# Differential attention on one core: five units in flight instead of two, with zero-padded 128-row queries as the stationary operand

## The reference, cut to what matters

```python
def one_block(q_blk):
    s = jnp.einsum('bmhqd,bmhkd->bmhqk', q_blk, k).astype(jnp.float32) * scale
    p = jax.nn.softmax(s, axis=-1)
    pd = (p[:, 0] - lam * p[:, 1]).astype(v.dtype)
    return jnp.einsum('bhqk,bhkd->bhqd', pd, v)
```

## Time and profile before

| what | us |
|---|---|
| median of 3 runs | 5201.45 |
| lowest and highest of them | 5197.71, 5202.65 |
| the profiled execution | 5201.73 |
| its span, first to last instruction | 5200.0 |

### The profile page before, as it was taken

How to read it: one execution, slowest core, us unless ns; L and a number is a source line. 1 busy time by engine, 2 the same in 40 slices (tenths; PEclk the granted TensorE clock), 3 DMA queues, 4 the chain that set the end, 5 groups by cost and what they waited for, 6 DMA issues and landing times. The chain is left out here.

```text
span 5200.0 us, 56901 instructions
## 1 busy us (share of the span) xinstructions
PE 4461.1 (86%) x20568; PEld 3190.8 (61%) x20568; DVE 3150.3 (61%) x6333; ACT 1600.8 (31%) x3153; POOL 754.9 (15%) x674
## 2 busy tenths in 40 slices
PE   7978998978999897698999999979977877877787
PEld 5635886744786584486888888867753333333333
DVE  5563223564322566666777777743548888888886
ACT  3233342332432223313555555533211111111111
POOL 0000110000110000100000000000014444444443
PEclk9978999978999899898999999999989989989989
DMA  3102331200333610131000000005239999999998
GB/s 117 36 1 77 97 97 60 81 1 33 106 97 127 236 42 2 57 125 51 12 14 14 14 13 14 3 18 173 89 113 421 417 410 410 414 412 407 416 408 356
DMA packets 141383, 778.75 MB, mean 150 GB/s; under 512 B 18692, under 2 KB 22164, under 8 KB 73000
## 3 DMA queue, kind: packets, MB, share of 16 engines
q0 software_dynamic: 80224, 565.16, 26.6%
q1 hardware_dynamic: 60872, 209.86, 12.1%
HBM read 755.04 MB, written 19.92 MB: 149 GB/s over the span
## 5 line engine op out<-in xcount | busy, mean ns | idle before, releaser
L2821 PE MATMUL psum<-rows,diag 128*128 128x512 f32 x2048 | 1018.9, 656 | 297.8 <-ACT diag L2800 292.8
L2821 PEld LDWEIGHTS psum<-rows,diag 128*128 128x128 f32 x2048 | 420.6, 211 | 878.0 <-issue 878.0
L419 DVE TENSOR_TENSOR w_split_lo<-w_raw,w_split_hi 128x1024 fp32r<-128x1024 f32 (+1 forms) x316 | 379.4, 1209 | 645.2 <-ACT w_split_hi L406 640.4
L2711 POOL DMA_INDIRECT rows<-in_peer_uv,sel_idx x512 | 618.9, 1209 | 932.2 <-PE psum L2821 634.2
L2726 DVE SCALAR_TENSOR_TENSOR uh<-rows,h_rows 128x1024 f32<-128x1024 f32 x512 | 627.9, 1226 | 180.5 <-DMA rows<-in_peer_uv,sel_idx 151.3
L406 ACT CAST w_split_hi<-w_raw 128x1024 fp32r<-128x1024 f32 (+1 forms) x316 | 322.6, 1028 | 817.6 <-PE psum L357 457.2
L2793 ACT ACTIVATE g<-g 128x4 f32<-128x4 f32 x128 | 26.3, 205 | 1077.9 <-DVE g L2737 1077.9
L592 POOL TENSOR_TENSOR uT_lo<-normed_rows,uT_hi 128x512 fp32r<-128x512 f32 x64 | 82.8, 1293 | 1377.8 <-ACT uT_hi L568 1377.8
L1901 PE MATMUL psum<-X_wide,wAT_wide 128*128 128x128 f32 x1920 | 254.6, 276 | 2.1 <-DVE X_wide L2247 1.8
L1901 PEld LDWEIGHTS psum<-X_wide,wAT_wide 128*128 128x128 f32 x1920 | 237.4, 192 | 19.1 <-issue 15.0
L1912 PE MATMUL psum<-U_wide,Y_wide 128*128 128x128 f32 x1536 | 202.1, 275 | 0.0
(11 more groups left out here) (495 smaller groups left out, 9310.4 us busy)
## 6 DMA issues: line engine op xcount, KB each, us to landing
w_raw<-in_w_in SPq DMA_DIRECT2D x120, 512.0 KB, 4.5
w_raw<-in_w_up SPq DMA_DIRECT2D x64, 512.0 KB, 4.3
w_raw<-in_w_down SPq DMA_DIRECT2D x64, 512.0 KB, 4.4
wbuf_mod<-in_w_mod SPq DMA_DIRECT2D x12, 2048.0 KB, 12.5
w_raw<-in_w_out SPq DMA_DIRECT2D x24, 512.0 KB, 4.7
w_raw<-in_peer_wq SPq DMA_DIRECT2D x16, 512.0 KB, 4.4
rows<-in_peer_uv,sel_idx POOLq DMA_INDIRECT x512, 13.0
w_raw<-in_w_branch_a SPq DMA_DIRECT2D x8, 512.0 KB, 4.1
```

Of the source, the lines that this page charges most:

```text
L419: nc.vector.tensor_tensor(ring.lo[:, q % SPLIT_RING, :, 0:w], raw[:, q % raw_ring, :, 0:w], ring.hi[:, q % SPLIT_RING, :, 0:w].bitcast(F32 ...
L2711: nc.gpsimd.indirect_dma_start(out=rows[:, n % RB, :], out_offset=None, in_=I["peer_uv"], in_offset=bass.IndirectOffsetOnAxis(ap=sel[:, t, ...
L2821: last = nc.tensor.matmul(psum[:, 2 * (t % 2) + half, :], diag[:, n % (2 * BATCH), :], rows[:, n % RB, D + half * NB:D + (half + 1) * NB], ...
```

## The change

It does the following.

1. `da_pr` holds four units in place of two, and the work is cut into finer steps with an order of its own on each engine. In step `i` of 37, PE does scores of map 0 of unit i, values(i-5), scores of map 1 of unit i, turn(i-3). DVE does the maximum of map 0 of unit i, difference(i-3), the maximum of map 1 of unit i, out(i-5), weights(i-1). ACT does the exponential of map 1 of unit i-1, copy(i-4), the exponential of map 0 of unit i, scale(i-2).
2. Each map has semaphores of its own, and each maximum is followed by a scaling of its own, so that an exponential waits for its own map alone.
3. The scaling of map 1 by its weight (128x768) moves from DVE to ACT. The square and its sum become one DVE operation with an accumulator.
4. For each unit and map, POOL copies the 64 rows of queries into one of four slots of `qp`, whose other 64 rows it set to zero once at the start. The scores are then products over 128 rows: the queries of the map with zeros below or above, against the keys of both maps.
5. `da_pT` and `qp` lie in the room of `x`.

```diff
-        pr = sb("da_pr", [P, 2, 2, N_ALL])
-        pT = sb("da_pT", [P, 2, N_ALL])
+        pr = sb("da_pr", [P, 4, 2, N_ALL])
+        room = T["x"][:].rearrange("p t d -> p (t d)")
+        pT = room[:, 0:2 * N_ALL].rearrange("p (i n) -> p i n", i=2)
+        qp = room[:, 2 * N_ALL:2 * N_ALL + 8 * P].rearrange("p (i m n) -> p i m n", i=4, m=2)
...
+            @block.gpsimd
+            def _(pool):
+                nc.gpsimd.memset(qp, 0.0).then_inc(pads_zero, 1)
+                pool.wait_ge(pads_zero, 1)
+                for u in range(UNITS):
+                    h, i = divmod(u, ST)
+                    for m in range(2):
+                        if u >= 4:
+                            pool.wait_ge(scores_ready[m], u - 3)
+                        mine = slice(64 * m, 64 * m + 64)
+                        nc.gpsimd.tensor_copy(qp[mine, u % 4, m, :], qT[mine, i, h, :]).then_inc(q_padded, 1)
...
                         if u >= 1:
-                            pe.wait_ge(probs_ready, 2 * (u - 1) + m + 1)
-                        lo = 64 * m
+                            pe.wait_ge(probs_ready[m], u)
+                        pe.wait_ge(q_padded, 2 * u + m + 1)
                         for a, b in ((0, 512), (512, N_ALL)):
-                            last = nc.tensor.matmul(S_of(m)[:, a:b], qT[lo:lo + 64, i, h, :],
-                                                    kT[lo:lo + 64, a // P:b // P, h, :], start=True, stop=True)
-                        last.then_inc(scores_ready, 1)
+                            last = nc.tensor.matmul(S_of(m)[:, a:b], qp[:, u % 4, m, :], kT[:, a // P:b // P, h, :],
+                                                    start=True, stop=True)
+                        last.then_inc(scores_ready[m], 1)
...
-                scores(0)
-                for u in range(UNITS + 1):
-                    if u + 1 < UNITS:
-                        scores(u + 1)
-                    if u < UNITS:
-                        turn(u)
-                    if u >= 1:
-                        values(u - 1)
+                for i in range(UNITS + 5):
+                    at(scores(0), i)
+                    at(values, i - 5)
+                    at(scores(1), i)
+                    at(turn, i - 3)
...
                 def difference(u):
-                    dve.wait_ge(probs_ready, 2 * u + 2)
-                    chain.after(nc.vector.reciprocal(ri[:, 0:2, u % 2:u % 2 + 1], ls[:, :, u:u + 1]))
-                    chain.after(nc.vector.tensor_tensor(ri[:, 2, u % 2:u % 2 + 1], ri[:, 1, u % 2:u % 2 + 1],
-                                                        lam["neg"][:], ALU.mult))
-                    p = pr[:, u % 2]
-                    chain.after(nc.vector.tensor_scalar(p[:, 1, :], p[:, 1, :], ri[:, 2, u % 2:u % 2 + 1], None,
-                                                        ALU.mult))
-                    nc.vector.scalar_tensor_tensor(p[:, 0, :], p[:, 0, :], ri[:, 0, u % 2:u % 2 + 1], p[:, 1, :],
+                    dve.wait_ge(scaled, u + 1)
+                    p = pr[:, u % 4]
+                    nc.vector.scalar_tensor_tensor(p[:, 0, :], p[:, 0, :], ri[:, 0, u % 4:u % 4 + 1], p[:, 1, :],
                                                    ALU.mult, ALU.add).then_inc(diff_ready, 1)
...
-                    chain.after(nc.vector.tensor_tensor(junk[:], o, o, ALU.mult))
-                    chain.after(nc.vector.reduce_sum(sq[:, 0, u:u + 1], junk[:], AX.X))
...
+                    chain.after(nc.vector.scalar_tensor_tensor(junk[:], o, 1.0, o, ALU.mult, ALU.mult,
+                                                               accum_out=sq[:, 0, u:u + 1]))
+
+                for i in range(UNITS + 5):
+                    at(maximum(0), i)
+                    at(difference, i - 3)
+                    at(maximum(1), i)
+                    at(out, i - 5)
+                    at(weights, i - 1)
...
+                def scale(u):
+                    act.wait_ge(weights_ready, u + 1)
+                    p1 = pr[:, u % 4, 1, :]
+                    nc.scalar.activation(p1, p1, ACT.Copy, scale=ri[:, 2, u % 4:u % 4 + 1]).then_inc(scaled, 1)
...
+                for i in range(UNITS + 5):
+                    at(probs(1), i - 1)
+                    at(copy, i - 4)
+                    at(probs(0), i)
+                    at(scale, i - 2)
```

More of the change, by code:

```diff
@@ L1573, in _, with maximum, step, weights @@
                 chain = Chain(dve, vec_step)
-                def maxima(u):
+                def maximum(m):
+                    def step(u):
+                        dve.wait_ge(scores_ready[m], u + 1)
+                        chain.after(nc.vector.tensor_reduce(nm[:, m, u:u + 1], S_of(m), AX.X, ALU.max, negate=True))
+                        nc.vector.tensor_scalar(nm[:, m, u:u + 1], nm[:, m, u:u + 1], SCALE, None, ALU.mult
+                                                ).then_inc(max_taken[m], 1)
+                    return step
+                def weights(u):
                     for m in range(2):
-                        dve.wait_ge(scores_ready, 2 * u + m + 1)
-                        chain.after(nc.vector.tensor_reduce(nm[:, m, u:u + 1], S_of(m), AX.X, ALU.max, negate=True))
-                    nc.vector.tensor_scalar(nm[:, :, u:u + 1], nm[:, :, u:u + 1], SCALE, None, ALU.mult
-                                            ).then_inc(max_taken, 1)
+                        dve.wait_ge(probs_ready[m], u + 1)
+                    chain.after(nc.vector.reciprocal(ri[:, 0:2, u % 4:u % 4 + 1], ls[:, :, u:u + 1]))
+                    nc.vector.tensor_tensor(ri[:, 2, u % 4:u % 4 + 1], ri[:, 1, u % 4:u % 4 + 1], lam["neg"][:],
+                                            ALU.mult).then_inc(weights_ready, 1)
                 def difference(u):
-                    dve.wait_ge(probs_ready, 2 * u + 2)
-                    chain.after(nc.vector.reciprocal(ri[:, 0:2, u % 2:u % 2 + 1], ls[:, :, u:u + 1]))
-                    chain.after(nc.vector.tensor_tensor(ri[:, 2, u % 2:u % 2 + 1], ri[:, 1, u % 2:u % 2 + 1],
-                                                        lam["neg"][:], ALU.mult))
-                    p = pr[:, u % 2]
-                    chain.after(nc.vector.tensor_scalar(p[:, 1, :], p[:, 1, :], ri[:, 2, u % 2:u % 2 + 1], None,
-                                                        ALU.mult))
-                    nc.vector.scalar_tensor_tensor(p[:, 0, :], p[:, 0, :], ri[:, 0, u % 2:u % 2 + 1], p[:, 1, :],
+                    dve.wait_ge(scaled, u + 1)
+                    p = pr[:, u % 4]
+                    nc.vector.scalar_tensor_tensor(p[:, 0, :], p[:, 0, :], ri[:, 0, u % 4:u % 4 + 1], p[:, 1, :],
                                                    ALU.mult, ALU.add).then_inc(diff_ready, 1)
@@ L1598, in out, with probs, step @@
                     dve.wait_ge(out_taken, u + 1)
-                    chain.after(nc.vector.tensor_tensor(junk[:], o, o, ALU.mult))
-                    chain.after(nc.vector.reduce_sum(sq[:, 0, u:u + 1], junk[:], AX.X))
-                maxima(0)
-                for u in range(UNITS + 1):
-                    if u < UNITS:
-                        difference(u)
-                    if u + 1 < UNITS:
-                        maxima(u + 1)
-                    if u >= 1:
-                        out(u - 1)
+                    chain.after(nc.vector.scalar_tensor_tensor(junk[:], o, 1.0, o, ALU.mult, ALU.mult,
[6 more added lines that the diff above has]
+                    at(weights, i - 1)
             @block.scalar
             def _(act):
-                def probs(u):
-                    act.wait_ge(max_taken, u + 1)
-                    if u >= 2:
-                        act.wait_ge(turned_ready, u - 1)
-                    for m in range(2):
-                        nc.scalar.activation(pr[:, u % 2, m, :], S_of(m), ACT.Exp, bias=nm[:, m, u:u + 1], scale=SCALE,
-                                             accum_out=ls[:, m, u:u + 1]).then_inc(probs_ready, 1)
+                def probs(m):
+                    def step(u):
+                        act.wait_ge(max_taken[m], u + 1)
+                        if u >= 4:
+                            act.wait_ge(turned_ready, u - 3)
+                        nc.scalar.activation(pr[:, u % 4, m, :], S_of(m), ACT.Exp, bias=nm[:, m, u:u + 1],
+                                             scale=SCALE, accum_out=ls[:, m, u:u + 1]).then_inc(probs_ready[m], 1)
+                    return step
+                def scale(u):
+                    act.wait_ge(weights_ready, u + 1)
+                    p1 = pr[:, u % 4, 1, :]
+                    nc.scalar.activation(p1, p1, ACT.Copy, scale=ri[:, 2, u % 4:u % 4 + 1]).then_inc(scaled, 1)
                 def copy(u):
@@ L1625, in copy @@
                     nc.scalar.copy(pT[:, u % 2, :], turned).then_inc(turned_copied, 1)
-                probs(0)
-                for u in range(UNITS):
-                    if u + 1 < UNITS:
-                        probs(u + 1)
```

(3 more changed lines are left out.)

26 lines of the change are left out of this document (17 added, 9 removed).

## The result

| | before | after |
|---|---|---|
| median of 4 runs, us | 5202.05 | 5156.39 |
| lowest and highest, us | 5197.71, 5203.92 | 5147.41, 5161.06 |
| the profiled execution, us | 5201.73 | 5147.41 |
| stage in it, first to last instruction, us | 207.2 | 157.4 |
| step (a unit) in it, us | 6.14 | 4.58 |

The ratio of after to before is 0.9906, with a 95% interval of 0.9894 to 0.9918: 45.7 us less by the medians. In the profiled executions the stage gives 49.8 us (POOL's memset included), and the rest of the span is 4.6 us shorter, 4992.8 against 4988.2. That rest differs from run to run: over the profiles of this study it lies between 4988 and 5002 us; I did not follow up why.

A forecast was written before the change was run, and what follows sets the result against it. A chain of waits, 6.14 us a unit, was taken as the bound. 31 steps of 4.7 (145.7), - 3 + 2.6, 1.4 for POOL and 17.8 draining give 164.5 us instead of 207.1, so 5201.7 - 42.6 = 5159; range 5149 to 5182.

The forecast's parts named there:

- The chain of 6.14 us: Old stage: waits through exponentials, small weight operations, scaling, difference and both maxima set each unit's 6.14 us, PE in none.
- PE's sum: PE's work per unit without waits: scores 2.58, values 1.33, turn 0.66, together 4.57 us.
- DVE's sum: DVE's work per unit: maxima, difference, output copy, small weight operations, two scalings of maxima, square and sum; 4.42 us.
- The wait of 0.2 before the turn: On PE, turn(i-3) behind map 1 waits 0.2 us for DVE's difference; mean step about 4.7 us.
- Scaling moved to ACT, at nothing: The 128x768 scaling takes 0.85 us on ACT, costing nothing while ACT has a third of the step free.
- POOL: Copies 0.3 us, hidden; start 1.4 us; contention 0 to 0.1 a step. Rival: POOL sets the step, 5230 us, chance 0.03.
- 64 against 128 rows: Score products: values between maps leave little overlap, so the sum stays; by half the argument 64-row scores save some 10 us.
- Filling and draining: Stage ends: first four steps some 3 us less, half-clock start adds 2.6, draining 17.8 us.
- the loop of one map: Single PSUM place per map: scores 1.50, maximum 0.985, its scaling 0.21, exponential 1.04; 3.74 us, below PE's and DVE's sums.
- Coupling: Rival: hops stand behind foreign operations on in-order engines; step 5.1 to 5.8, time 5171 to 5193 us, chance 0.13.
- no effect: Rival: steps stay near 6.1 us and the deeper pipeline only fills longer; 5202 us, chance 0.05.
- half clock: Rival: TensorE stays at half clock, PE's 4.57 becomes 9.1 us a step; 5296 us, chance 0.02.

The follow-up runs named there:

- the other order with padding: Changed kernel with both maps' scores adjacent on PE, then values, turn; DVE and ACT reordered, padded scores and POOL copies kept; ratio 0.9900.
- the other order 64-row maps without any padding: Changed kernel without POOL and padding, both maps' 64-row scores adjacent on PE, then values, turn; DVE and ACT reordered; 5153.11 us, ratio 0.9906.
- the 64-row kernel: Changed kernel with both maps' scores as 64-row products, no POOL padding, values still between the maps; ten runs, median 5189.54 us, ratio 0.9981.
- The six padded units: Kernel with adjacent 64-row maps, but the first six units' scores padded to 128 rows by POOL; 5145.60 us, ratio 0.9886 to the kernel before.

## Why the prediction was right, point by point

- **What bounds the kernel now**: right. The chain of 6.14 us went, and the padding alone, which touches only PE's work, moved no step of it. That PE's work sets the new step is shown by the run with half the values, which shortened it, and by the other order with padding, which did not change it.
- **PE's sum**: 4.57 forecast, 4.58 measured, to a hundredth in each part.
- **DVE's sum**: 4.42 forecast, 4.06 measured. The mis-sized terms are the small operations that are not waited for. A scaling of a maximum cost 0.07 (2049.63 to 2049.70) and not 0.19, since the next operation starts before it ends; the last weight operation 0.08 and not 0.20; square and sum 0.33 with the accumulator read inside, not 0.41. The earlier trace rows showed this overlap once, in the difference (1.02 long, 0.94 to the next), and I used it there alone. There it was not due: a wait stands behind the difference now, and it counts in full, 1.01. DVE's idle time is 0.52 us a step where I had 0.2 to 0.3.
- **The wait of 0.2 before the turn**, from which I made 4.7 of 4.57: it did not come. The loop through that wait takes 4.34 us with DVE's real times, shorter than PE's sum. The loop is real, as the runs with the scaling on DVE (4.99) and with half the values (4.33) show, but it only binds when PE does not. Over 31 steps of 0.12 this is 3.7 us.
- **Scaling moved to ACT, at nothing**: right in the changed kernel, though it takes 0.93 and not 0.85. Taken back it costs 0.41 us a step, 13.4 us in the stage.
- **POOL**: copies 0.29 (0.3 forecast), first score 1.35 us after the memset's start (1.4). The 0 to 0.1 us a step for contention is 0: the difference takes 1.01, and took 1.02 with POOL idle.
- **64 against 128 rows**: here the text was wrong on what it compared with. It said that 64-row scores in this order would leave the sum as it is, or save 10 us. They cost 0.73 us a step and tens of us at half clock, some 33 us of the median. So of the 46 us gained by the change, the order without the padding gives some 15 by the medians of ten and thirteen runs (1 to 19 by the interval of the ratio), and in this order the rest needs the padding, which no term of my sum shows. In the other order 64-row maps without any padding reach the same time. Of the two statements cited from the Trainium skill, "TensorEngine Tiling (Array Packing)", section Key Properties, the traces agree with both: a change of array shape costs 0.18 to 0.2 us, though no row shows the drain itself, and tiles of different rows run side by side where they are adjacent (1.80 or 2.37 us for a pair). Which one decides is a matter of the order around them.
- **Filling and draining**: the first steps took 3.82 us (3.74 forecast for the loop of one map). From the first score to the map-0 scores of the last unit (1967.99 to 2108.60) it took 140.6 us where I had 145.3. Of the 4.7 between them, 3.7 are the wait above, and 1.1 the half clock at the start: full clock came within the first pair of maps, so the first maximum came 2.97 us after the first score and not 1.50, 1.5 us lost where I had 2.6. The drain from there to the end took 15.5 us where I had 17.8. The clock stayed full in it (1.00 in the window from 2112), so the 2 us that I set aside for the clock were not due. With 1.35 for POOL the stage was 157.4, not 164.5.
- **The sum**: 42.6 us forecast, 45.7 measured by medians. That they agree better than the stage (42.6 against 49.8) is the noise of the rest of the span, and so luck: timed again, beside other kernels, the change gave 50.7 us by medians. The forecast of the stage was 7 us too long, by the three terms named. The range was also uneven: a step of 4.57 gives 5159 - 31 x 0.13 = 5155, and not the 5150 that I put at the lower end of the forecast case.
- **Coupling**, the second case: not in this kernel, but one step less in flight gives 5.57, as that rival had it. The other rivals (POOL, no effect, half clock) did not occur; half clock occurred in the 64-row kernel.

## What to carry to other kernels

Work out each engine's sum of work from start-to-start distances, and beside it each loop through the in-order lists: in these runs the largest of all was the step. PE's sum was forecast to a hundredth of a us (4.57 and 4.58). The loops (4.99, 5.57) were read off the runs in which they bind, and one was carried over to another run (4.34 and 4.33). A busy share of 100% is not enough to tell which it is; cut some of the engine's work and see whether the step follows. A reordering that fills PE also fills it with every cost that waits used to hide; here the changes between 64-row and 128-row products, free while PE idled, would have eaten, with the half clock that came with them, some two thirds of the gain. Either pad them away or put products of different rows next to each other, and look at the granted clock of the first tens of us.

## What the runs showed of the hardware that I had not expected

- TensorE at half clock while busy all the time. In the 64-row kernel with parted maps, PE was busy 60.00 of 60.00 us at a granted clock of 0.50 (1.2 GHz), and later 80.00 of 80.00 at 1.00. In all nine profiles of the new orders with at least one padded map of a unit at the start, the clock was full within 7 us of the first score; in the three profiles of kernels with 64-row scores in the new orders it took from 21 to 103 us, in two of them with a brief rise before. In the old order the rows made no difference: the kernel before, with 64-row scores, was granted 0.50 up to 1976.0 and 1.00 from 1976.3, 11 us after its first score, and with the padding alone it took 12 us. So 64 rows alone don't decide it. What does was not settled: I compared whole kernels, and did not vary PE's pauses by themselves. The six padded units removed the low clock in the one profile taken, and the runs then spread by 4 us.
- A change between 64-row and 128-row products costs PE 0.18 us on average where a step has four (5.31 against 4.58) and 0.20 where it has two (4.97 against 4.58).
- DVE operations without a wait between them start 0.08 us before the one ahead ends, a small one (0.15 long, 0.07 to the next) as well as a large one (1.02 long, 0.94 to the next).
- POOL copies of one input beside DVE's difference, which reads two inputs in SBUF, cost it nothing (1008 ns), with POOL busy for 51.5 of 122 us.
